# Cross attention in three passes of rounded part and rest, on one core

## What is computed

```python
h = rmsnorm(x, g)                      # 512 x 1024
q = h @ wq                             # 4 heads of 256
k, v = split(rmsnorm(mem) @ wkv)       # 256 memory rows
s = einsum("bthd,bmhd->bhtm", q, k) * 256 ** -0.5
p = softmax(s, axis=-1)
x = x + einsum("bhtm,bmhd->bthd", p, v).reshape(...) @ wo
```

## Time and profile before

| | us |
|---|---|
| median of 3 runs (2478.20 to 2478.91) | 2478.65 |
| the profiled execution, own time | 2479.44 |
| its span | 2477.5 |
| PE busy | 2412.6 |
| VectorE, ScalarE, GpSimd busy | 1234.2, 966.8, 999.2 |

### The profile page before, as it was taken

One profiled execution on the slowest core, in us unless ns is written; L12 is line 12 of the kernel. 1 busy time (PEld: TensorE's weight loads), 2 busy tenths in 40 slices (PEclk: granted clock), 3 DMA queues, 4 the chain that ended last, 5 costly groups with the idle time before them and its releaser, 6 DMA issues.

```text
span 2477.5 us, 30080 instructions
## 1 busy us (share of the span) xinstructions
PE 2412.6 (97%) x11174; PEld 1909.6 (77%) x11174; DVE 1234.2 (50%) x2086; ACT 966.8 (39%) x1455; POOL 999.2 (40%) x744
## 2 busy tenths in 40 slices
PE   7999999999999999999999999999999999999998
PEld 6777667977888888758868888887566977888887
DVE  4353445324333336694356555556764334545555
ACT  4345344433322226524444222226765433322223
POOL 3423324242445445535424544554021232544543
PEclk9999999999999999999999999999999999999999
DMA  5222213431332333222213223222102421222231
GB/s 164 71 69 81 70 55 119 136 102 38 120 99 88 102 102 97 92 68 86 85 56 102 88 99 102 97 90 66 35 18 85 139 99 51 88 99 94 93 102 69
DMA packets 176732, 217.86 MB, mean 88 GB/s; under 512 B 6568, under 2 KB 157658, under 8 KB 176614
## 3 DMA queue, kind: packets, MB, share of 16 engines
q1 hardware_dynamic: 175446, 214.16, 26.7%
q10 hardware_dynamic: 1168, 2.11, 0.3%
HBM read 214.14 MB, written 2.12 MB: 87 GB/s over the span
## 4 chain that ended last, share of the span: by engine, by line
PE 90%; DVE 4%; ACT 3%; issue 2%; POOL 1%; DMA 0%; DVEq 0%; SPq 0%; ACTq 0%
PE ps_l L782 77%; PE ps_l L993 3%; PE ps_l L1116 2%; PE ps_l L904 2%; PE ps_s L1043 1%; ACT w_hi L1323 1%; PE ps_s L1179 1%; PE ps_s L1099 1%; POOL w_lo L633 1%; DVE arena L1913 1%; DVE a_lo L1919 1%; PE ps_s L1194 1%; PE ps_s L1008 1%; DVE x_T L2226 0%; DVE small L2616 0%
## 5 line engine op out<-in xcount | busy, mean ns | idle before, releaser
L633 POOL TENSOR_TENSOR w_lo<-w_raw,w_hi 128x512 fp32r<-128x512 f32 (+1 forms) x740 | 999.0, 1381 | 1452.1 <-ACT w_hi L1323 1442.0
L782 PE MATMUL ps_l<-a_hi,w_hi 128*128 128x512 f32 x1936 | 766.1, 396 | 11.9 <-DVE b_lo L2247 7.9
L782 PE MATMUL ps_l<-a_lo,w_hi 128*128 128x512 f32 x1952 | 761.0, 391 | 0.0
L782 PE MATMUL ps_l<-a_hi,w_lo 128*128 128x512 f32 x1936 | 756.2, 391 | 0.0
L1323 ACT ACTIVATE w_hi<-w_raw 128x2048 fp32r<-128x2048 f32 x197 | 372.4, 1890 | 571.1 <-PE ps_l L782 556.2
L782 PEld LDWEIGHTS ps_l<-a_hi,w_hi 128*128 128x128 f32 x1936 | 364.6, 188 | 97.8 <-DVE b_lo L2247 8.4
L782 PEld LDWEIGHTS ps_l<-a_lo,w_hi 128*128 128x128 f32 x1952 | 367.9, 188 | 79.1 <-issue 3.1
L782 PEld LDWEIGHTS ps_l<-a_hi,w_lo 128*128 128x128 f32 x1936 | 364.0, 188 | 77.5
L782 PE MATMUL ps_l<-b_hi,w_hi 128*128 128x512 f32 (+1 forms) x908 | 336.0, 370 | 8.4 <-POOL w_lo L633 3.2
L782 PE MATMUL ps_l<-b_lo,w_hi 128*128 128x512 f32 (+1 forms) x908 | 333.3, 367 | 0.0
L782 PE MATMUL ps_l<-b_hi,w_lo 128*128 128x512 f32 (+1 forms) x908 | 333.3, 367 | 0.0
(11 more groups left out here) (274 smaller groups left out, 2612.4 us busy)
## 6 DMA issues: line engine op xcount, KB each, us to landing
w_raw<-in_ffn_w_up_dram SPq DMA_DIRECT2D x44, 1024.0 KB, 5.1
w_raw<-in_w_dram SPq DMA_DIRECT2D x32, 1024.0 KB, 5.1
w_raw<-in_ffn_w_down_dram SPq DMA_DIRECT2D x22, 1024.0 KB, 4.9
w_raw<-in_w_in_dram SPq DMA_DIRECT2D x20, 1024.0 KB, 5.4
w_raw<-in_xa_wkv_dram SPq DMA_DIRECT2D x16, 1024.0 KB, 5.6
w_raw<-in_w_kv_mem_dram SPq DMA_DIRECT2D x8, 1024.0 KB, 5.7
w_raw<-in_xa_wq_dram SPq DMA_DIRECT2D x8, 1024.0 KB, 5.0
w_raw<-in_xa_wo_dram SPq DMA_DIRECT2D x8, 1024.0 KB, 5.1
```

The source lines that it names most:

```text
L633: e.tensor_tensor(w_lo[:, b % 2, o], w_raw[:, b % 2, o], w_hi[:, b % 2, o].bitcast(F32), ALU.subtract).then_inc(w_lo_made[by], 1)
L782: ins = pe.matmul(o, *((v, w) if swap else (w, v)), start=first and n == 0, stop=last and n == 2)
```

## The change

The scores and the value products of the three cross attentions are made by `mm3`. For that ACT writes rounded queries to `A_hi` and DVE the rests to `A_lo`; keys and values get a rounded and a rest copy as well (directly out of PSUM for c = 0, 2, by two whole-tile copies and two whole-tile subtractions during `xq1` for c = 1). The turned probabilities are rounded by ACT into `B_hi`, and DVE subtracts for `B_lo`, which now frees the bank. The queries are no longer multiplied by 1/rms: the sums of squares are made as columns (`norm_columns`, lines 885 and 886, in place of `norm`, lines 874 and 875), ACT makes `rcol` of them, and `rcol` is the scale of the exponential and of the negated maximum. The turn T(s - 3) stands ahead of V and O in its step. Semaphore counts follow.

```diff
@@ attention_events, in each step of the event list (also `turn_first` as a new argument, True for the three xa)
+        turn = [("T", *divmod(step - lag, TT))] if lag <= step < n + lag else []
+        if turn_first:
+            ev += turn
         for kind in "VOMN":
             if (step, kind) in due and (kind in "VO" or "M" in extra):
                 ev.append((kind, due[step, kind], 0))
-        if lag <= step < n + lag:
-            h, i = divmod(step - lag, TT)
-            ev.append(("T", h, i))
+        if not turn_first:
+            ev += turn
@@ make_plan: who frees the PSUM groups
-        feat(f"xk{c}", wkv, "a", [0, 256, 512, 768], low_by="ppvv")
+        feat(f"xk{c}", wkv, "v", [0, 256, 512, 768], low_by="ppvv")
-        L.add(f"xv{c}{j}", "aa")
+        L.add(f"xv{c}{j}", "aa" if c == 1 else "vv")
-        norm({0: 1, 1: 5, 2: 8}[c])
+        S.add(f"cols{(1, 5, 8)[c]}", "a")
-        attention(f"xa{c}", XA_HEADS, 3, "a", 1, v_groups=2)
+        attention(f"xa{c}", XA_HEADS, 3, "a", 1, t_who="v", v_groups=2, turn_first=True)
@@ tensor, cross
-                stage(f"xq{c}", x2, ready=h_ready(k_norm), behind={0: lambda: norm(k_norm)})
+                stage(f"xq{c}", x2, ready=h_ready(k_norm), behind={0: lambda: norm_columns(k_norm)})
@@ score
+                    if c == 1 and h == 0 and i == 0:
+                        pe.wait_ge(kv_lo, 2)
                     for d in (0, 1):
-                        ins = pe.matmul(bank(S, g)[:, 0:MEM], qT[:, 2 * h + d, i * P:(i + 1) * P],
-                                        kT[:, 2 * h + d, :], start=d == 0, stop=d == 1)
+                        n, o = 2 * h + d, slice(i * P, (i + 1) * P)
+                        ins = mm3(bank(S, g)[:, 0:MEM], A_hi[:, n, o], A_lo[:, n, o], kh_m[:, n, :], kl_m[:, n, :],
+                                  d == 0, d == 1)
@@ values
-                            ins = pe.matmul(bank(L, g + d)[:, :], vM[:, m, h * 256 + d * P:h * 256 + (d + 1) * P],
-                                            ptx(h)[:, m, :], start=m == 0, stop=m == MT - 1)
+                            ins = mm3(bank(L, g + d)[:, :], vh_m[:, m, o], vl_m[:, m, o], ptx(B_hi, h)[:, m, :],
+                                      ptx(B_lo, h)[:, m, :], m == 0, m == MT - 1)
@@ scalar, cross
+            def query_rstd(k):
+                g = S.base[f"cols{k}"]
+                act.preload_act_table_set("natural_log_exp_and_others")
+                wait_group(act, S, g)
+                act.activation(rcol, bank(S, g)[:, 0:TT], ACT.Ln, bias=eps256, scale=256.0 / D).then_inc(s_free["a"], 1)
+                wait_read(act, S, g)
+                act.activation(rcol, rcol, ACT.Exp, scale=-0.5).then_inc(rq_r, 1)
...
                 if c != 1:
-                    mem_keys(c)
+                    for j in range(4):
+                        key_parts(c, j)
                     for v in range(4):
-                        mem_values(c, v)()
-                norm_rstd(k_norm)
-                just_hi(f"xq{c}", 4)
+                        mem_hi_parts(c, f"xv{c}{v}", lambda q: vh_m[:, q, 256 * v:256 * v + 256])
+                b, g = plan.block_base[f"xq{c}"], L.base[f"xq{c}"]
+                for j in range(4):
+                    for n in (2 * j, 2 * j + 1):
+                        wait_group(act, L, g + n)
+                        act.activation(A_hi[:, n, :], bank(L, g + n)[:, :], ACT.Copy).then_inc(q_hi, 1)
+                    hi(b + j + 2)
+                    if j == 0:
+                        query_rstd(k_norm)
+                    if c == 1 and j < 2:
+                        act.activation((vh_m if j else kh_m)[:, :, :], (vM if j else kT)[:, :, :], ACT.Copy).then_inc(kv_hi, 1)
@@ copy of a turn, and the exponential
-                    act.activation(ptx(h)[:, :, i * P:(i + 1) * P], tiles, ACT.Copy).then_inc(l_free["a"], 1)
+                    act.activation(ptx(B_hi, h, slice(i * P, (i + 1) * P)), tiles, ACT.Copy).then_inc(t_hi, 1)
-                                       scale=1 / 16, accum_out=ls[:, u % 8:u % 8 + 1]).then_inc(s_free["a"], 1)
+                                       scale=rcol[:, i:i + 1], accum_out=ls[:, u % 8:u % 8 + 1]).then_inc(s_free["a"], 1)
@@ vector, cross: mem_low(j) subtracts the rounded part from the two groups of block j, as turned below
-                    for early in range(4):
-                        low_part(dve, b - 4 + early)
-                    low_part(dve, b)
-                    low_part(dve, b + 1)
-                dve.wait_ge(n_rstd, k_norm + 1)
-                scaled(L.base[f"xq{c}"], 8, lambda j: qT[:, j, :])
+                    b = plan.block_base[f"xk{c}"] + 2
+                    for j in range(8):
+                        if j < 6:
+                            low_part(dve, b + j)
+                        mem_low(j)
+                g = L.base[f"xq{c}"]
+                for n in range(KD):
+                    wait_group(dve, L, g + n)
+                    dve.wait_ge(q_hi, KD * c + n + 1)
+                    dve.tensor_tensor(A_lo[:, n, :], bank(L, g + n)[:, :], A_hi[:, n, :].bitcast(F32), ALU.subtract)\
+                        .then_inc(l_free["v"], 1)
+                    if c == 1 and n in (3, 5):
+                        dve.wait_ge(kv_hi, KVB[1] + n // 2)
+                        whole, hi_t, lo_t = (vM, vh_m, vl_m) if n == 5 else (kT, kh_m, kl_m)
+                        dve.tensor_tensor(lo_t[:, :, :], whole[:, :, :], hi_t[:, :, :].bitcast(F32), ALU.subtract)\
+                            .then_inc(kv_lo, 1)
+                dve.wait_ge(rq_r, c + 1)
@@ scores: the negated maximum
-                    dve.tensor_scalar(nm[:, u % 8:u % 8 + 1], mx[:, u % 8:u % 8 + 1], -1 / 16, None, ALU.mult)\
-                        .then_inc(u_nm, 1)
+                    dve.tensor_scalar(nm[:, u % 8:u % 8 + 1], mx[:, u % 8:u % 8 + 1], rcol[:, i:i + 1], -1.0,
+                                      ALU.mult, ALU.mult).then_inc(u_nm, 1)
+                def turned(g, h, i):
+                    o = slice(i * P, (i + 1) * P)
+                    tiles = bank(L, g)[:, 0:MEM].rearrange("p (m q) -> p m q", q=P)
+                    wait_group(dve, L, g)
+                    dve.wait_ge(t_hi, XA_HEADS * TT * c + TT * h + i + 1)
+                    dve.tensor_tensor(ptx(B_lo, h, o), tiles, ptx(B_hi, h, o).bitcast(F32), ALU.subtract)\
+                        .then_inc(l_free["v"], 1)
@@ walk, at each event of VectorE, after the values of P
+                    if kind == "T" and turned:
+                        turned(g, h, i)
```

More of the change, by code:

```diff
@@ L86, in lin, with attention_events @@
     return i * by + (f(1) - by) if by else f(1)
-def attention_events(heads, lag, extra, after, fill):
+def attention_events(heads, lag, extra, after, fill, turn_first=False):
     ev = []
@@ L109, in attention_events @@
                 ev.append((kind, due[step, kind], 0))
-        if lag <= step < n + lag:
-            h, i = divmod(step - lag, TT)
-            ev.append(("T", h, i))
+        if not turn_first:
+            ev += turn
+        if turn:
+            _, h, i = turn[0]
             if i == TT - 1:
@@ L178, in attention @@
     def attention(name, heads, lag, score_who, per_score, t_who="a", v_who="v", v_groups=1, extra="",
-                  after=(3, 3, 4, 3, 3), fills=()):
+                  after=(3, 3, 4, 3, 3), fills=(), turn_first=False):
         fill = {}
@@ L184, in attention @@
                 fill.setdefault(step, []).append((tag, *divmod(n, parts), parts))
-        ev = attention_events(heads, lag, extra, after, fill)
+        ev = attention_events(heads, lag, extra, after, fill, turn_first)
         at = {}
@@ L350 @@
 OH = {"diff": 0, "fox": 4, "xa0": 12, "xa1": 20, "mla0": 28, "mla1": 36, "xa2": 44}
+KVB = (0, 16, 18)
 UPB = {"mlp": 0, "ffn0": 32, "ffn1": 54}
@@ L357, in n_base, with sums_before, rstd_count @@
     return 8 * k - (8 if k > 3 else 0)
+def sums_before(k):
+    return {1: "cols0", 2: "cols1", 5: "norm3", 6: "cols5", 9: "cols8"}.get(k, f"norm{k - 1}")
+def rstd_count(k):
+    return sum(n <= k for n in (0, 2, 3, 4, 6, 7, 9))
 def sum_base(k):
@@ L512, in build, with ptx @@
         p_x = ar(0, 4, MEM)
-        def ptx(h):
-            return ar(1024 + 1024 * (h % 2), MT, T)
+        def ptx(part, h, o=slice(0, T)):
+            return part[:, 2 * (h % 2):2 * (h % 2) + 2, o]
         r32, f32 = ar(R0, 2, T), ar(R0 + 1024, 2, T)
@@ L1569, in _, with mem_hi_parts @@
             squares_and_z("w_o", 4, 1, lambda: mem_parts(0))
-            def mem_keys(c):
-                block_copies(f"xk{c}", 4, 2, lambda j: kT[:, j, :], cols=MEM)
+            def mem_hi_parts(c, name, dst):
+                for q in (0, 1):
+                    wait_group(act, L, L.base[name] + q)
+                    act.activation(dst(q), bank(L, L.base[name] + q)[:, 0:MEM], ACT.Copy).then_inc(kv_hi, 1)
+                hi(plan.block_base[name] + 2)
             def key_copies(c, j):
@@ L2094, in plain_norm, with walk @@
```

(14 more changed lines are left out.)

43 lines of the change are left out of this document (32 added, 11 removed).

## The result

The changed kernel takes 2503.47 us (median of 4 runs, 2499.13 to 2505.38) against 2478.78 us in the runs of the kernel before beside them: ratio 1.0096, 95% interval 1.0084 to 1.0108. It is slower, by 24.7 us, where 14.1 were forecast. The profiled execution took 2504.5 us, of which 2502.7 is its span. The mean granted clock is 0.988 (0.994 before).

The account below looks back on a forecast made before the run. PE nearly full before; after the change a ring between VectorE and ScalarE sets the attentions' pace. Three attentions at 4.5 us give 13.5, keys 0.6: 14.1 slower, 2492.8 us on the median of 2478.65; own range 2486 to 2501, stated range 2481 to 2506.

Parts of the forecast that it names:

- signs of being wrong: Profile after: turns 1.3 us apart, clock under 1.00 in the attentions, or PE waits in the key blocks beyond 0.3 us.
- The ring: Attentions: maximum, negated maximum, exponential, ScalarE's copy, VectorE's rest and next maximum wait on each other, 2.05 us per unit.
- Length of one attention: Last query group to `xo`, 35.2 us before: steps 0.5 + 3.5 + 0 + 1.4 - 1.0, 4.4, say 4.5 us longer.
- the 0.5 of the late start: Last query group to first turn: queries' rounded copy delays the first exponential by 0.51 us, 3.55 becomes 4.06.
- The first three steps of the table: Each attention: first turn to values 0, 10.8 us; values 0 to values 1, 8.7; values 1 to values 2, 8.7.
- values 2 to `xo`: Attention's end, values of head 2 to output projection: 8.37 us before, 7.4 forecast, 1.0 shorter.
- The clock: Rival: PE's clock falls at the values, 2.72 becomes 5.44 us; once per attention 8 us, 2501; four times 2525; chance 0.13.
- The forecast's own case: Ring sets the pace in the attentions with the clock staying up: 14.1 us slower, chance 0.64.
- Keys: Key projections of c = 0 and 2: VectorE frees banks behind a weight block's rest, 0.3 us later, twice.
- unexpected stall in the keys: Key blocks: a case outside the forecast and its rivals, chance 0.04.
- Turns ahead of the values: Attentions: without this order rests stand behind the values' 2.72 us on PE in each head, two us more per attention.
- PE's busy time: Three-pass scores and values on PE: 5.1 us less per attention, 15 us less in all.

Follow-up runs that it names:

- cut at two places: Changed kernel with VectorE's rest of the turned tile behind the next maximum, 2491.35 us; changed kernel with ScalarE's copy ahead of the exponential, 2487.36 us.
- shortened at a third: Changed kernel with the constant 1/16 instead of the 1/rms pointer in the exponential and the negated maximum: 2497.62 us.
- the fed run: Changed kernel with six added 256-column matmuls on PE before its wait at 11 turns of each attention: 2497.97 us.
- both traces: The changed kernel's first profiled execution, 2504.5 us, and that of the same kernel unaltered, measured again at 2504.9 us.
- the run: Changed kernel with each step's turn behind the values again, output rests of P ahead of the turned tile's rest: 2506.75 us.
- the last version but one: Changed kernel with VectorE's rest behind the next maximum, turns four units and values four steps behind, keys' and values' rests ahead of weights' rests: 2476.97 us.

## Why the prediction was right, and where it wasn't

The time lies in the range, 10.7 us above the point. It lies above the 2486 to 2501 that the forecast allowed its own terms, and inside the stated range because that reached up to 2506 for one fall of the clock per attention. Two of its own signs of being wrong came: a clock under 1.00 in the attentions and a wait of PE beyond 0.3 us in the key blocks. So the place and the size of the ring were foreseen, most of the rest of the 24.7 us was not, and that the range took that in was in part luck. (The lower end of 2486 was added up wrongly as well: 1.2, 0.6 and 1.2, three times, are 9.0 below 2492.8, thus 2484.) By its own steps:

- **The ring** was right in place and in size: 2.05 forecast, 2.07 measured, each piece within 0.02 us (rest to next maximum 0.34 for 0.33, maximum to negated maximum 0.45, exponential 0.56 long). It was cut at two places and shortened at a third, and each time the attention followed. The two cuts took 12 and 16 us off the whole.
- **Length of one attention:** 4.4 forecast with the 0.5 of the late start. At full clock (the fed run's attentions) the stretches are 4.5, 4.5 and 4.85 us longer, and the start, ahead of the stretch, 0.47: 5.0 to 5.3 together, 0.6 to 0.9 short. The first three steps of the table hold within 0.1; "values 2 to `xo`" was 0.6 too short: the second group of the values was full at 3.0 and not 2.9 us, and VectorE reached the last turn's rest, behind both output rests, later than added up: its 0.43 began at 2080.64, 4.7 us after the values' start, where the sum had it end then.
- **The clock** is the term that was missing. The rival was there, with its place (the values) and its chance of 0.13, and it was priced at 8 us for one fall in each attention. It came true in two attentions of three, in both traces, in the profiled one for 2.6 and 3.1 us, 5.7 together. The forecast's own case left it out because PE was busy 54% in the ring and a stretch of 54% had kept its clock. That step failed twice. In the ring proper PE was busy 2.31 of 4.00 us from 547 to 551, 58%, and the clock fell at 551 all the same. And the average was taken over the wrong stretch: in the ring a fall cost nothing in the first attention and 0.5 us in the second (it reached the values of head 0), and the one that costs more comes after the last scores, where PE is busy 1.03 of 4.00 us, a smaller share than the 1.21 of 3.00 at which it fell before. This could be seen ahead: the forecast names the place where the last scores run out before values 2, and took no average over it. The Trainium skill, TensorE: Matmul & The Clock Gate, section "HAM oscillation — how this bites in real kernels", lays such falls to idle gaps, each longer than any wait of PE in these attentions. From 566 to 574 us, ahead of the fall, PE's longest single wait was 1.6 us, so here the measurement decides against that reading: shorter waits were enough in this attention, and in the third the same ones were not.
- **Keys:** 0.3 twice forecast. In the first cross attention it was 0.3 or less. (By the forecast's own terms it is 0.42 + 0.1 - 0.15 = 0.37, which it rounded down.) In the third PE waited 2.6 us, a late transfer that was 1.3 us longer than before and no effect of the order; the 0.04 kept for an unexpected stall in the keys named no cause and had no price in the sum.
- **Turns ahead of the values:** "two us more per attention" without them was wrong, it is 0.9 at most, by one attention of the run. The step counted the ring's stand at each head in full and nothing for the step of 2.57 that is there anyway.
- **PE's busy time** down 15 us: 4.4 in the third attention, where 5.1 were forecast for one, but half clock stretches the records elsewhere, and the sum over the kernel hides it. Busy time at a changing clock isn't an amount of work.

The sum of the profiled execution's 25.2 us of span: the attentions' ring 4.5 + 4.5 + 4.85 = 13.8, their late starts 3 x 0.47 = 1.4, the clock in them 5.7, and 4.3 elsewhere. Of these 4.3, the late transfer of keys and the half-clock stretch behind it make about 3; the rest are half-clock stretches in unchanged code between the attentions, some that before has and some that it hasn't. That code is the same, so they depend on when it is reached or vary by execution; which of the two was not tried.

## What to carry to other kernels

Two in-order engines that hand pieces to each other both ways within one unit make a ring, and its turn, not the sum of either engine's work, sets the pace: write the two lists side by side and look for an instruction of unit u + 1 that is queued behind one that needs unit u. It was cut here by moving one instruction in one list. A deeper distance between the stages then took another 4.8 us off each attention (50.2 to 45.4), part of it by a clock that no longer fell. When PE is going to wait, look ahead to what it does next: idle time just before a long stretch of matmuls can be paid twice, once as wait and once as half clock.

## What the runs showed that I had not expected

- 198 added matmuls of 256 columns, in PE's waits, made the kernel 5.5 us faster (2503.47 to 2497.97), by keeping the granted clock at 1.00.
- One half-clock stretch cost 1.5 us (46.93 against 45.41) where it met the values, and nothing (52.86 against 52.85) where it met mostly waits.
- Half-clock stretches came in unchanged code in one kernel and not in another: the 12 us from 1700 on have a mean clock of 0.86 in the changed kernel, and the same code has 1.00 before, while the one that before has at 1810 is missing in the changed kernel. Single runs of one kernel lie 6 to 8 us apart (before 2476.66 to 2482.91, the last version but one 2471.69 to 2479.87), and a gain of 7.8 us in the attentions arrived as 3.6 in the profiled execution and as 2.4 between the medians.
- The transfer of one 1 MB block of weights took 6.28 us before and 7.57 us in the changed kernel, with nothing altered about it.
